# Modulation sums in eight wide matmuls and a transpose on TensorE, in place of 32 narrow ones and a transpose on VectorE

## The reference, cut to what matters

```python
def adaln(cond, w, b):
    return jnp.split(jax.nn.silu(cond) @ w + b, 6, axis=-1)

def layer(x, ctx, c, c_ctx, w_ada, b_ada, ...):
    sh1, sc1, gt1, sh2, sc2, gt2 = [m[:, None, :] for m in adaln(c, w_ada, b_ada)]
    csh1, csc1, cgt1, csh2, csc2, cgt2 = adaln(c_ctx, w_ada, b_ada)
```

## Time and profile before

| | |
|---|---|
| median of 3 runs | 2782.18 us (2780.88 to 2782.61) |
| the profiled execution | 2782.61 us, span 2780.8 us |
| PE busy | 2670.1 us, 96% of the span |
| PEld busy | 2426.1 us, 87% |
| DVE busy | 1390.0 us, 50% |
| ACT busy | 543.7 us, 20% |
| granted TensorE clock, mean | 0.985 of full speed |

### The profile page before, as it was taken

The page is one execution under the profiler, slowest core; times in us unless marked ns, Lnnn a source line. Parts: engine busy times, 40 slices in busy tenths (PEclk is TensorE's granted clock), DMA queues, the critical chain, the costliest instruction groups (busy, mean ns, idle before and its releaser), DMA issues.

```text
span 2780.8 us, 50617 instructions
## 1 busy us (share of the span) xinstructions
PE 2670.1 (96%) x20834; PEld 2426.1 (87%) x20834; DVE 1390.0 (50%) x2269; ACT 543.7 (20%) x1139; POOL 8.5 (0%) x19
## 2 busy tenths in 40 slices
PE   6999999999999999999999999899997899988999
PEld 6999778988999999787988999769995699956999
DVE  5554255324665655235521655246662566615665
ACT  2111132111111111123120111231112321123111
POOL 0000000000000000000000000000000000000000
PEclk9999999999999999999999999999999999999999
DMA  6654321135555655331125565423434134431342
GB/s 250 223 206 162 114 107 46 56 127 194 204 215 207 228 198 208 130 121 51 47 87 201 199 228 201 156 93 127 177 122 155 63 134 171 173 131 55 128 182 107
DMA packets 50176, 416.12 MB, mean 150 GB/s; under 512 B 4016, under 2 KB 4272, under 8 KB 29584
## 3 DMA queue, kind: packets, MB, share of 16 engines
q1 hardware_dynamic: 49344, 409.34, 39.9%
q0 software_dynamic: 592, 3.41, 0.3%
HBM read 411.69 MB, written 1.05 MB: 148 GB/s over the span
## 4 chain that ended last, share of the span: by engine, by line
PE 92%; DVE 4%; ACT 2%; issue 1%; DVEq 1%; DMA 0%; ACTq 0%; SPq 0%
PE units L721 29%; PE spots L721 22%; PE units L671 21%; PE spots L985 4%; PE units L1096 2%; PE spots L702 2%; PE units L1141 1%; PE units L1234 1%; PE units L790 1%; PE spots L1175 1%; PE units L1137 1%; PE spots L1165 1%; PE spots L1156 1%; PE spots L859 0%; PE spots L882 0%
## 5 line engine op out<-in xcount | busy, mean ns | idle before, releaser
L671 PE MATMUL units<-normed,weights 128*128 128x256 f32 x2016 | 455.5, 385 | 20.4 <-ACT normed L1302 11.3
L671 PEld LDWEIGHTS units<-normed,weights 128*128 128x128 f32 x2016 | 384.1, 192 | 83.9 <-issue 13.6
L721 PE MATMUL units<-normed,weights 128*128 128x128 f32 x2176 | 274.5, 280 | 19.6 <-DVE normed L1679 13.4
L721 PEld LDWEIGHTS units<-normed,weights 128*128 128x128 f32 x2176 | 259.2, 194 | 26.6 <-DVE normed L1679 15.3
L721 PE MATMUL spots<-normed,weights 128*128 128x128 f32 x2176 | 268.1, 277 | 0.0
L721 PEld LDWEIGHTS spots<-normed,weights 128*128 128x128 f32 x2176 | 257.2, 194 | 0.0
L1302 ACT ACTIVATE mla_q_rope<-units 128x256 f32<-128x256 f32 (+1 forms) x248 | 95.5, 387 | 611.8 <-PE units L721 574.9
L1796 DVE TENSOR_TENSOR delta_new_values<-spots,mla_q_rope 128x256 f32<-128x256 f32 x116 | 49.2, 425 | 277.5 <-PE spots L721 277.5
L721 PE MATMUL units<-hidden,weights 128*128 128x128 f32 x1472 | 180.9, 276 | 0.0
L721 PE MATMUL spots<-hidden,weights 128*128 128x128 f32 x1472 | 180.1, 275 | 0.0
L721 PEld LDWEIGHTS units<-hidden,weights 128*128 128x128 f32 x1472 | 172.0, 192 | 1.6 <-issue 1.6
(11 more groups left out here) (324 smaller groups left out, 3482.5 us busy)
## 6 DMA issues: line engine op xcount, KB each, us to landing
weights<-stream SPq DMA_DIRECT2D x140, 2048.0 KB, 7.8
values_mla_qk_mla_values<-stream SPq DMA_DIRECT2D x24, 2048.0 KB, 8.4
weights<-stream SPq DMA_DIRECT2D x46, 1024.0 KB, 5.1
weights<-stream SPq DMA_DIRECT2D x16, 768.0 KB, 5.5
constants<-consts SPq DMA_DIRECT2D x1, 1094.5 KB, 8.3
residual<-x_in SPq DMA_DIRECT2D x1, 1024.0 KB, 5.0
weights<-stream SPq DMA_DIRECT2D x4, 256.0 KB, 5.6
conv_in<-ctx_in POOLq DMA_DIRECT2D x1, 1024.0 KB, 5.1
```

Source lines behind the costliest of these rows:

```text
L671: mm = pe.matmul(dst, w[:, kt * width + col:kt * width + col + P], rhs[:, kt, :], start=(kt == 0), stop=(kt == k - 1))
L721: mm = pe.matmul(dst[:, m * P:m * P + P], weights[:, m, kt, :], moving(kt), start=(first and m == 0 and kt == 0), stop=(kt == n - 1), skip ...
```

## The change

The sums of a piece are made by eight matmuls in place of 32: one for each `kt`, on all 512 columns at once, into the strip `q = kt % 4`. So a strip holds the sum of two `kt` only, and the four strips' partial results still have to be added. ScalarE copies the 128 x 512 result from PSUM to `ada_s` (`ada_copy`). Then TensorE runs four more matmuls (`ada_turn`), with 128x128 of that copy as weights and two columns of constants as moving operand; these columns pick row `j` of each strip, so that the matmul adds the four strips and puts features on partitions at once. VectorE's transpose goes, and the bias is added straight from PSUM. `ada_turn(k)` stands on TensorE after `end(k)`, four quarters after the sums; `ada_copy` stands on ScalarE after the copy to `u4s` and ahead of `keep_c1(k+1)`. Two semaphores are new, and `load_ada` now waits for the sums of the piece before (`ada_summed`) in place of a count of finished spots.

```diff
@@ sync
-            for signal_ in (*lin_taken, *spot_taken, spot_ready, c11_made, c21_made):
+            for signal_ in (*lin_taken, *spot_taken, spot_ready, ada_summed, c11_made, c21_made):
@@ load_ada
-                    before_ = SPOT["one"]["ada", i - 1][0][0] + 1 if i else 0
-                    sp.wait_ge(*(merged_made.at(c, 4) if i == ADAS else spot_ready.at(c, before_)))
+                    sp.wait_ge(*(merged_made.at(c, 4) if i == ADAS else ada_summed.at(c, i)))
@@ tensor: ada_sums, ada_turn, multiply
                 for kt in range(KD):
-                    for q in range(4):
-                        w = vqv[:, kt * 512:kt * 512 + 512].rearrange("p (m c) -> p m c", m=4)[:, :, 32 * q:32 * q + 32]
-                        mm = pe.matmul(banks[32 * q:32 * q + 32, 0, 0:P], cond_s[:, kt, :], w, start=(kt == 0),
-                                       stop=(kt == KD - 1))
+                    q = kt % 4
+                    mm = pe.matmul(banks[32 * q:32 * q + 32, 1, :], cond_s[:, kt, :], vqv[:, kt * 512:kt * 512 + 512],
+                                   start=(kt < 4), stop=(kt >= 4))
+                mm.then_inc(ada_summed.handle, 1)
+
+            def ada_turn(c, i):
+
+                pe.wait_ge(*ada_copied.at(c, i + 1))
+                _, banks, _ = spot_of(c, ("ada", i))
+                for m in range(4):
+                    mm = pe.matmul(banks[:, 0, 2 * m:2 * m + 2], ada_s[:, i % 2, m * P:m * P + P],
+                                   cst[:, C_TWO:C_TWO + 2], start=True, stop=True)
                 mm.then_inc(spot_ready.handle, 1)
...
                     end(k)
+                    if c.sec == "one" and k in ADA_AT:
+                        ada_turn(c, ADAS * which + ADA_AT.index(k))
@@ scalar: ada_copy, multiply
+            def ada_copy(c, i):
+                e_.wait_ge(*ada_summed.at(c, i + 1))
+                if i >= 2:
+                    e_.wait_ge(*spot_ready.at(c, SPOT[c.sec]["ada", i - 2][0][0] + 1))
+                _, banks, _ = spot_of(c, ("ada", i))
+                activate(ada_s[:, i % 2, :], banks[:, 1, :], ACT.Copy).then_inc(ada_copied.handle, 1)
...
                     activate(u4s[k % 2], lin[:, k % 2, 0:T], ACT.Copy).then_inc(u4_kept.handle, 1)
+                    if c.sec == "one" and k in ADA_AT:
+                        ada_copy(c, ADAS * which + ADA_AT.index(k))
                     if k + 1 < count:
                         keep_c1(k + 1)
@@ vector: ada_bias
-                ve.transpose(ada_s[:, i % 2, 0:P], banks[:, 0, 0:P]).then_inc(free, 1)
-                ve.drain()
-                turned = ada_s[:, i % 2, 0:P].rearrange("p (m j) -> p m j", m=4)[:, :, 0:2]
-                ve.tensor_tensor(mod[:, m, :], turned, bias_a[:, m].unsqueeze(2).to_broadcast([P, 4, 2]), ALU.add)
+                ve.tensor_tensor(mod[:, m, :], banks[:, 0, 0:8].rearrange("p (m j) -> p m j", m=4),
+                                 bias_a[:, m].unsqueeze(2).to_broadcast([P, 4, 2]), ALU.add).then_inc(free, 1)
```

More of the change, by code:

```diff
@@ L380, in build @@
         ada_loaded = signal("ada_weights_loaded", one=16 * ADA_TURN)
+        ada_summed = signal("ada_summed", 1, one=ADA_TURN)
+        ada_copied = signal("ada_copied", one=ADA_TURN)
         p1_done, p2_done, p4_done, p5_done, p6_done, p7_done = (signal(f"product{i}_done", **MUS) for i in (1, 2, 4, 5, 6, 7))
```

## The result

| | before | after |
|---|---|---|
| median, us | 2781.53 (2779.88 to 2782.61, 4 runs) | 2806.38 (2804.60 to 2810.24, 4 runs) |
| ratio | 1 | 1.0092 [1.0080, 1.0105] |
| profiled execution: time, span, us | 2782.61, 2780.8 | 2807.2, 2805.4 |
| mean granted clock | 0.985 | 0.984 |

The change makes the kernel slower by 24.85 us. The forecast was 2800, with a range of 2791 to 2808. The page of the kernel after: its span, what each engine was busy, and the chain that ended last.

What follows compares the result with a forecast made beforehand. TensorE was taken to bound the kernel (96% of span, 92% of chain). Turns 17.8, three ends 1.4, one at 0 and sums -1.2 made +18.0 us on 2782.61: predicted 2800, range 2791 to 2808.

Steps and rivals of the forecast that it cites:

- the sum: Whole kernel: 20 turns x 0.89 = 17.8, three at 0.47 = 1.4, one at 0, sums -1.2: +18.0 us.
- Part 1: A piece's sums on TensorE: four rounds of four overlapping strips, 1.72 us against 1.79; taken as -0.05 us a piece.
- Rival A: Sums on TensorE: strips don't overlap on 512 columns, +140 us, 2922; by program-order starts +69, 2851; chance of either 0.05.
- Part 2: The turn on TensorE: 8 records paced by loading fp32 weights, 0.89 us a turn, bounds 0.54 and 1.1.
- Rivals B: The turn on TensorE is cheaper: weights load at the lighter pace, 0.54 us a turn; +10, 2792 us; chance 0.07.
- C (0.06): The turn on TensorE is nearly free, weight loads not holding so narrow a matmul: 0.06 us, total 2782; chance 0.02.
- Parts 3 and 4: ScalarE's 0.60 us copy hidden behind the next quarter, cost 0; VectorE loses its transpose and drain, effect 0.
- Part 4: VectorE: 0.6 us x 24 taken off where TensorE isn't waiting, 0; down steps wait some 0.5 us for the turn, 0.
- Part 5: Ends of MLPs: three of four cost 0.47 us in place of 0.89; the fourth, between the loop's turns, 0.
- Part 6: SP's queue at the loop boundary: three transfers go up to 6 us earlier; nothing on TensorE waits, so 0.
- rival D: Whole kernel's clock: stretches at half clock, 42 us lost, shift and decide the sign; about 2782 us, chance 0.04.
- The allowance of 2 us: Clock term in the range: 2 us added at the high end, with turns of 1.1 us, giving 2808.

## Why the prediction was right, and where it was short

The direction and the main mechanism, eight weight loads in the turn, were right, and the result lies in the range; the forecast was 6 us low. That the range held is in part luck: its high end came from a turn of 1.1 us, and the turn took 0.89. Two losses that the sum put at nothing, 2.5 and 3.05 us, took up that room.

Part 1, the sums: forecast -0.05 a piece, measured -0.03. Rival A is out: the four strips overlap on 512 columns, and they do so even in the order that by the rule of the Trainium skill should have been worst.

Part 2, the turn: forecast 0.89, measured 0.89 between quarters. The argument was that half the columns save nothing from 128 to 64, so the weights set the pace. Rivals B (0.54) and C (0.06) are out; with 64 columns the turn costs the same, and without it the interval is back. The estimate from the Trainium skill's page TensorEngine Tiling (Array Packing), section Instruction Overhead, was 0.2; the traces have 0.89 with 2 columns and with 64, so a floor on the moving side isn't what binds here.

Parts 3 and 4, ScalarE and VectorE: both hidden, as forecast. The wait of the addition in down steps was forecast at some 0.5 each; VectorE in fact waited for the turn 4 times in all, 2.3 us together, at the last step of the MLPs, and nothing on TensorE followed from it. But Part 4 priced the work that was taken from VectorE and not the code. The program got 12 transposes and 12 drains shorter, and with that VectorE's stop ahead of the second block's MLP grew from 3.85 to 8.63 us: 3.05 us in the trace, after what the vanished delay of ScalarE gave back.

Part 5, the ends: three at 0.47 forecast, 0.34 measured. The squares' sum started 0.78 and not 0.89 later, and L693, which follows without a stop, took 1.89 in place of 1.99. The fourth at 0 is right for the turn alone (+0.15 with SP's old wait).

Part 6, SP's queue: this is the step that failed. "Nothing on TensorE waits for them there" is true, and the transfers were still not free, because they now fall on the 3.00 us in which VectorE restarts the loop. The row was quoted in the prediction ("3.00 by issue") and taken as fixed. Measured from the last piece to TensorE's restart: +2.46 in after and +0.15 with SP's old wait, so 2.3 for the early transfers, and +2.6 in the kernel before with that wait alone.

The clock, rival D: the mean grant of the profiled execution went from 0.985 to 0.984, so the clock did not turn the sign. The allowance of 2 us was too narrow for what one execution differs from the next: 21 runs of the kernel before on one chip lay between 2778.91 and 2785.05. It is also no independent item: behind the longer stop in the second block the time at half the clock is 10.2 us in place of 6.8.

The sum: 17.2 for the intervals (forecast 20 x 0.84 = 16.8), 1.0 for three ends (1.4), 2.5 at the fourth end (0), and 3.05 in the second block, which had no term. With both stops undone 18.6 are left (15.6 to 23.4), for a forecast of 18.0; so close an agreement is partly chance, since that kernel also has the gain by ScalarE and a wide spread. What stays open: why the code length alone moved the median so little, so how the 5.3 us divide between the two causes in the medians isn't settled; why ScalarE's delay went; and that a fetch behind weight transfers is the mechanism at the boundary, which is inferred from the queues and from when the fetch comes.

## What to carry to other kernels

In this kernel a matmul that brings its own full 128x128 fp32 weights cost 0.22 us of TensorE's queue (two records of 0.11), whether it streamed 2, 64 or 128 columns. On a queue that is 96% busy, a transpose on a half idle engine is the better place; if it must be a matmul, bf16 weights cost a fifth here, and the values are rounded. An idle time that the profile ends by "issue", at a loop's restart or at the entry to another part of the program, wasn't a constant here: look at which transfers the change puts beside it and at whose code it lengthens or shortens. When an engine's stop grows by 4.8 us and the engine behind it loses 1.55, look for the third one that had ended last before. Before taking a piece of work away from a place, ask what it covers there.

## What the hardware showed that was not expected

- VectorE's stop at the loop's restart is 3.0 to 3.3 us where SP issues its transfers after the squares' sum, and 5.4 to 6.4 where 2 MB transfers are already under way; at the entry to the second block's MLP code it is 3.2 to 3.9 us or 8.4 to 9.1, by 12 transposes and 12 drains in VectorE's code elsewhere. The sign is not that more code costs: the shorter program was the slow one.
- At that entry ScalarE started 3.4 to 4.4 us after VectorE's first result in the four traces with ScalarE's program of before, and 0.52 in the nine with the longer one.
- Matmuls in different strips of 32 columns start together though the program lists both matmuls of a strip in a row: 1.88 us for the sums against 1.86.
- The turn costs 0.89 with 2 and with 64 columns in fp32 and 0.17 in bf16, for half the passes a fifth of the time.
